# Opening stage of a recurrent-and-attention decoder: ScalarE issues two loads, TensorE sums all squares of x and runs unread products around the sums

## What is computed

```python
def rms_norm(x, gain, eps=RMS_EPS):
    xf = x.astype(jnp.float32)
    y = xf * lax.rsqrt(jnp.mean(xf * xf, axis=-1, keepdims=True) + eps)
    return (y * gain).astype(x.dtype)
...
h = rms_norm(x, mix_norm[layer])
...
xx = jnp.pad(h, ((0, 0), (1, 0), (0, 0)))[:, :-1] - h
x_mix = h[None] + xx[None] * mu[:, None, None, :]
rkv = jnp.einsum('cbsd,cde->cbse', x_mix[:3], w_rkv)
```

## Time and profile before

| what | us |
|---|---|
| median of 3 runs | 1757.51 |
| lowest and highest | 1757.46, 1759.23 |
| profiled execution, its own time | 1756.64 |
| its span, first to last instruction | 1754.6 |
| TensorE busy in the span | 1737.8 |

### The profile page before, as it was taken

The page is one execution under the profiler, slowest core; times in us unless marked ns, Lnnn a source line. Parts: engine busy times, 40 slices in busy tenths (PEclk is TensorE's granted clock), DMA queues, the critical chain, the costliest instruction groups (busy, mean ns, idle before and its releaser), DMA issues.

```text
span 1754.6 us, 35883 instructions
## 1 busy us (share of the span) xinstructions
PE 1737.8 (99%) x15388; PEld 1351.8 (77%) x15388; DVE 898.3 (51%) x1566; ACT 740.4 (42%) x1285; POOL 197.9 (11%) x172
## 2 busy tenths in 40 slices
PE   7999999999999999999999999999999999999999
PEld 3756666666578888888888888888888888888887
DVE  7835555564554444333456655655665544444321
ACT  6434444532332222223565565565565522222211
POOL 0033443441000000000111111111110000000000
PEclk8999999999999999999999999999999999999999
DMA  4321111121244444433332322222322233233332
GB/s 143 97 69 31 34 33 46 42 66 43 73 143 133 132 132 132 132 96 96 99 94 76 93 79 79 85 85 73 97 73 73 73 107 97 96 97 96 96 96 96
DMA packets 59174, 155.00 MB, mean 88 GB/s; under 512 B 7224, under 2 KB 24168, under 8 KB 59017
## 3 DMA queue, kind: packets, MB, share of 16 engines
q1 hardware_dynamic: 58920, 152.63, 27.9%
q10 hardware_dynamic: 96, 0.07, 0.0%
HBM read 150.51 MB, written 11.61 MB: 92 GB/s over the span
## 4 chain that ended last, share of the span: by engine, by line
PE 98%; DVE 0%; DMA 0%; issue 0%; SPq 0%; ACT 0%; DVEq 0%
PE bank L635 96%; PE bank L638 3%; DMA f<-xT 0%; SPq L510 0%; DVE f L2063 0%; DVE f L1956 0%; DVE f L2065 0%; DVE f L1866 0%; DVE f L2052 0%; ACT f L1431 0%; DVE f L2210 0%; DVE f L2428 0%; ACT f L1433 0%; ACT f L1443 0%; DVE f L1992 0%
## 5 line engine op out<-in xcount | busy, mean ns | idle before, releaser
L635 PE MATMUL bank<-r 128*128 128x512 f32 x5424 | 1252.2, 391 | 0.7 <-DVE f L2215 0.7
L635 PEld LDWEIGHTS bank<-r 128*128 128x128 f32 x5424 | 1013.3, 188 | 218.1 <-issue 6.6
L635 PE MATMUL bank<-f 64*64 64x64 f32 (+6 forms) x9532 | 456.3, 279 | 13.0 <-ACT f L1443 4.4
L1842 DVE TENSOR_TENSOR r<-f,r 128x1024 fp32r<-128x1024 f32 x222 | 280.8, 1265 | 361.2 <-ACT r L1418 361.2
L635 PEld LDWEIGHTS bank<-f 64*64 64x64 f32 (+3 forms) x9532 | 290.5, 138 | 170.4 <-issue 106.7
L1418 ACT ACTIVATE r<-f 128x1024 fp32r<-128x1024 f32 x222 | 232.5, 1048 | 146.0 <-PE bank L635 142.3
L2541 POOL TENSOR_TENSOR r<-f,r 128x512 fp32r<-128x512 f32 x48 | 63.8, 1328 | 805.1 <-ACT r L1730 805.1
L1709 ACT ACTIVATE r<-f 128x512 fp32r<-128x512 f32 x44 | 27.8, 632 | 213.5 <-DVE f L2222 213.5
L2252 DVE TENSOR_TENSOR f<-bank,f 128x512 f32<-128x512 f32 x72 | 56.0, 778 | 80.8 <-PE bank L635 78.1
L1741 ACT ACTIVATE f<-bank,f 128x512 f32<-128x512 f32 x48 | 33.0, 689 | 104.0 <-PE bank L635 103.2
L1706 ACT ACTIVATE f<-f 128x512 f32<-128x512 f32 x44 | 27.8, 632 | 110.1 <-DVE f L2210 110.1
(11 more groups left out here) (119 smaller groups left out, 923.3 us busy)
## 6 DMA issues: line engine op xcount, KB each, us to landing
f<-stream SPq DMA_DIRECT2D x246, 512.0 KB, 3.6
bias_copies<-bias_rows SPq DMA_DIRECT2D x48, 192.0 KB, 3.7
f<-xT SPq DMA_DIRECT2D x16, 256.0 KB, 4.3
f<-lora_out SPq DMA_DIRECT2D x16, 128.0 KB, 3.4
f<-bias_copies SPq DMA_DIRECT2D x64, 32.0 KB, 2.4
f<-bias_copies SPq DMA_DIRECT2D x32, 64.0 KB, 2.1
outT<-f SPq DMA_DIRECT2D x8, 256.0 KB, 4.5
f<-const SPq DMA_DIRECT2D x1, 576.0 KB, 4.8
```

The lines of the kernel that those rows point to most:

```text
L635: return nc.tensor.matmul(out, lhsT, rhs, start=start, stop=stop, skip_group_check=True)
L1842: TT(r(lo_at(q), 1024), f(raw_of(panel_of(q)), 1024), rf(hi_at(q), 1024), ALU.subtract).then_inc(s["w_lo"], 1)
```

## The change

SyncE's queue loses the loads of the ones and of the vectors; ScalarE issues them at the head of its own, ahead of the table of functions. VectorE clears 256 columns of the later value mix's place (`O_MIXV`) first, and no longer adds squares. TensorE starts with four products of that cleared block by itself into bank 6 (two records each, 256 columns of data), which nothing reads; then it sums all eight squares itself, makes the three bias products, and then runs eight products of the ones by the ones (128 columns of data, two records each), again into bank 6 and unread, ahead of the key.

```diff
@@ block.sync
             for k in range(KC):
                 sp.dma_start(hk(k), xT[k * P:(k + 1) * P, :]).then_inc(s[f"x_in{k}"], 16)
-                if k == 0:
-                    sp.dma_start(con(C_ONES), const[:, C_ONES:C_ONES + P]).then_inc(s["ones_in"], 16)
-                if k == 1:
-                    sp.dma_start(f(O_PV, N_PV), pvec).then_inc(s["vec_in"], 16)
@@ block.tensor
+            pe.wait_ge(s["pad"], 1)
+            for k in range(4):
+                mm(banks[6][:, 0:256], f(O_MIXV, P), f(O_MIXV, 256))
             pe.wait_ge(s["ones_in"], 16)
-            for k in range(2):
+            for k in range(KC):
                 pe.wait_ge(s["sq"], k + 1)
-                mm(NORM_SUM[:, :], con(C_ONES), f(x_square(k)), k == 0, False)
-            pe.wait_ge(s["x_sq_sum"], KC - 3)
-            mm(NORM_SUM[:, :], con(C_ONES), f(x_square(2)), False, True).then_inc(s["x_norm_ps"], 1)
+                last = mm(NORM_SUM[:, :], con(C_ONES), f(x_square(k)), k == 0, k == KC - 1)
+            last.then_inc(s["x_norm_ps"], 1)
             pe.wait_ge(s["oh_in"], 32)
             for g in range(3):
                 mm(banks[2 + g][0:16, 0:384], f(O_REL + 16 * g, 16, 0, 33),
                    f(O_OH + 384 * g, 384, 0, 33)).then_inc(s["bias_ps"], 1)
+
+            for k in range(8):
+                mm(banks[6][:, 0:P], con(C_ONES), con(C_ONES))
@@ block.scalar
+            act.dma_start(con(C_ONES), const[:, C_ONES:C_ONES + P]).then_inc(s["ones_in"], 16)
+            act.dma_start(f(O_PV, N_PV), pvec).then_inc(s["vec_in"], 16)
             exp_ln_tables()
@@ block.vector
+            V.memset(f(O_MIXV, 256), 0.0).then_inc(s["pad"], 1)
             for k in range(KC):
                 V.memset(f(O_H + k * (S + 1), 1), 0.0).then_inc(s["pad"], 1)
...
-            for k in range(3, KC):
-                dve.wait_ge(s["sq"], k + 1)
-                if k > 3:
-                    dve.wait_ge(s["x_sq_sum"], k - 3)
-                TT(f(x_square(2)), f(x_square(2)), f(x_square(k)), ALU.add).then_inc(s["x_sq_sum"], 1)
             dve.wait_ge(s["rstd"], 1)
-            dve.wait_ge(s["pad"], KC)
+            dve.wait_ge(s["pad"], KC + 1)
```

## The result

The changed kernel takes 1763.37 us (median of 6 runs) where the kernel before takes 1757.57 (6 runs): a ratio of 1.0031, 95% interval 1.0021 to 1.0040. It is slower, by 5.8 us, and the prediction of 1754.5 (1753.2 to 1756.3) was wrong. The profiled execution took 1763.76, with a span of 1761.8.

The account below looks back on a forecast made before the run. TensorE, busy 99% of the span, was taken to bound the kernel. The smaller of two opening gains, 2.15 us (logarithm) against 3.1 (TensorE done with the key), off 1756.64 gave 1754.5 us, range 1753.2 to 1756.3.

Parts of the forecast that it names:

- what the opening gives should reach the end: After the opening: no later DMA has a share in the chain, so time won there shortens the whole kernel.
- 3.4, 8 x 0.86, 2.3 us: TensorE's opening: running times of unread products ahead, eight squares at full clock, and 16 unread records behind the sums.
- D: After the opening: rival that the gain is lost at a transfer TensorE doesn't pace, 1756.6 us; chance 0.05.
- The logarithm 2.15 us earlier: Opening: the logarithm starts at about 12.65 against 14.80, with 0.9 and 2.8 us as ends.
- 6.2 taken: Opening: time in us at which TensorE's clock rises, the middle taken between 4.1 and 8.7.
- The last x at 10.7: Opening: with two loads moved to ScalarE, the last x lands at 10.7 us, between 10.23 and 11.18.
- Unread products behind, 2.3 us, key at 16.9: After the bias products: 16 unread records at 0.145 take 2.3 us; the key starts at 16.9 against 18.59.
- VectorE as the limit at the second receptance tile: Near 46 us: VectorE is level with TensorE, so the logarithm's 2.15 us counts, not TensorE's 3.1.
- Rival A: Second receptance tile: VectorE's chain is not the limit, TensorE's larger gain counts, 1753.0 to 1753.5 us; chance 0.18.
- B: Opening: rival that the clock rises late, winning 0 to 0.9 us, 1755.7 to 1756.6; chance 0.10.
- C: Opening: rival that the sums run at half clock throughout, key 8.7 us later, 1765.3 us; chance 0.04.
- 1754.5 as the sum of the opening: Whole kernel: the profiled execution's 1756.64 us less the smaller saving, 2.15, gives 1754.5; forecast chance 0.63.

Follow-up runs that it names:

- run of 1754.96: Changed kernel with its added products made up to 64 (256 instructions) by five more sums, seven large unread and 52 small products: 1754.96 us against 1757.61, ratio 0.9984.
- 1754.24: Changed kernel made up to 256 instructions, large unread products kept ahead of the sums (3, plus 24 small), those behind replaced by 32 small: 1754.24 us against 1756.80.

## Why the prediction was wrong

*Which step failed.* "The page's chain has no DMA later that amounts to a share, so what the opening gives should reach the end." It reached 130 us and was then outweighed by pauses of TensorE in code that nobody had touched. The unread products and the sums were priced by their own running time alone (3.4, 8 x 0.86, 2.3 us); that they move 31,000 later instructions by 68 places against the loads of 256 had no term. In its place the runs showed 9.6 us of pauses in the recurrent stage of the changed kernel (1.3 before), and 7.0 us of loss from the shift by 68 instructions alone. None of the four rivals held it either: D lost the gain at a transfer of data, and ended at 1756.6.

*Could it have been seen?* In part. The trace of before has four such pauses, with 1.3 us, and 66 of its 123 instruction loads lie between 130 and 450 us. So it was to be seen that whatever adds instructions ahead of that stage puts 66 places anew. That a place can cost over a microsecond was not: the largest pause there was 0.4. The Trainium skill's "Runtime: NRT & Kernel Launch", section "Instruction fetch mechanics", says that instructions are refilled in blocks of 16 KiB, 256 instructions, and that crossing a block's end is mostly hidden. The first half agrees with the trace (16.4 KB a load, pauses 256 records apart); the second doesn't hold where TensorE runs small products densely: up to 1.4 us at one end in the changed kernel, 9.6 in all.

*The logarithm 2.15 us earlier*: 2.28. The clock rose at about 6.0 (6.2 taken). That all-zero products raise it was open; they do. In the run of 1754.96 the trace's clock record has the rise at 4.2, and the first square's weight loads come at 5.3 us; without the large ones it rose at 10.4.

*The last x at 10.7*: 9.69, below the lower bound of 10.23. The bound took off the whole issue time of the two loads, 0.95; x came 1.5 earlier than before, and what gave the rest is not known. It didn't matter, for the sums stood in TensorE's queue without a break up to 12.25. In the traces the move does bring x earlier (the last square starts at 9.5 to 10.0 in the four executions with large products ahead and the loads on ScalarE, at 11.1 with them back in SyncE's queue), but it was worth nothing that the totals show.

*Unread products behind, 2.3 us, key at 16.9*: the 16 records took 0.11 each, 1.8 in all, and the key started at 16.3, right at its mix. The row of 0.145 was the mean of eight runs of eight products, which also follow each other at 0.11; the rest of it is the end of each run's last product.

*VectorE as the limit at the second receptance tile*: right. TensorE gained 2.2 to 2.3 there, as much as the logarithm and no more, and a key at half clock, in the run without large products behind, cost 0.3 to 0.5 us of its 1.7. Rival A falls. Rivals B and C fall in the changed kernel; B's late clock was seen only in the run without the large products ahead.

*1754.5 as the sum of the opening*: 1754.96 and 1754.24 with the shift undone. That they lie so near is partly luck. In their profiled executions the opening gave 2.9 and 1.4 us in place of 2.15, and the recurrent stage took 1.3 from the one and added 0.7 to the other.

What stays open: no record names the wait. That a pause is TensorE waiting for its next 256 instructions rests on its place, on the time from the load's end (1.2 to 1.6 us in 37 of 37 pauses) and on the runs with other shifts. When such a load is triggered, and why the pauses differ from execution to execution (6.1 us in the run with products at the end, 9.6 in the changed kernel, at the same places), was not tried. What each part of the opening is worth is open too, for the stage behind it varies by as much.

## What to carry to other kernels

An edit that adds or removes instructions on TensorE moves all later code against the places where its instructions are loaded; where small products follow densely, that alone can cost several microseconds (7.0 in this kernel), more than this opening wins. So compare such an edit with a version that is filled up to a multiple of 256 instructions by small unread products in an idle stretch, before judging it. Look at what the filling does where it stands, too: with 64 small products in the kernel before, the opening of the profiled execution ended 0.8 us later; why was not tried. In the trace, look for an engine's pauses that end with "issue", count the records between them, and compare their ends with the packets of the queue of instruction loads.

## What the runs showed of the hardware

TensorE paused at places 256 instructions apart, up to 1.8 us at one of them (in the run with 17 small products), and went on 1.2 to 1.6 us after the end of an instruction load. The total over one stage went from 1.3 to 9.0 us by a shift of 68 instructions, and to 1.0 by one of 256. With large products of zeros ahead, the clock rose at 4.2 to 7.2 us in the five profiled executions (6.0 in the changed kernel); with 51 small ones of 32x32 weights and then the sums, at 10.4.
